# S5 scan in chunks: four units fed at once into eight banks, states read in pairs, and the gate in the same block

## The reference, cut to what matters

```python
bu_re = jnp.einsum('bsgh,gph->bsgp', uf, bb_re)
bu_im = jnp.einsum('bsgh,gph->bsgp', uf, bb_im)
_, _, xr, xi = lax.associative_scan(combine, (a_re_t, a_im_t, bu_re, bu_im), axis=1)
y = (jnp.einsum('bsgp,ghp->bsgh', xr, c_re)
     - jnp.einsum('bsgp,ghp->bsgh', xi, c_im))
y = y.reshape(bsz, seq, S5_WIDTH) + d_skip * uf.reshape(bsz, seq, S5_WIDTH)
y = jax.nn.gelu(y, approximate=False)
y = y * jax.nn.sigmoid(y @ w_glu + b_glu)
```

## Time and profile before

| | us |
|---|---|
| median of 3 timed runs | 2995.52 |
| lowest, highest | 2992.05, 3009.61 |
| profiled execution | 2989.28 |
| its span | 2987.5 |
| mean granted clock of TensorE in it | 0.955 |

### The profile page before, as it was taken

The page is one execution under the profiler, slowest core; times in us unless marked ns, Lnnn a source line. Parts: engine busy times, 40 slices in busy tenths (PEclk is TensorE's granted clock), DMA queues, the critical chain, the costliest instruction groups (busy, mean ns, idle before and its releaser), DMA issues. The chain is left out here.

```text
span 2987.5 us, 38641 instructions
## 1 busy us (share of the span) xinstructions
PE 2740.0 (92%) x14085; PEld 2295.0 (77%) x14085; DVE 1947.1 (65%) x3130; ACT 1037.2 (35%) x1635; POOL 1283.5 (43%) x607
## 2 busy tenths in 40 slices
PE   7998999778989998979988999998999969999996
PEld 5887877336778887758876789998999958888785
DVE  5444232683454444366555267778999969999998
ACT  4232321453233223222022233334655524444342
POOL 3443442002434443423042356773222247777773
PEclk9999999699999999989798999999999989999998
DMA  5443341002234443322002245557999999999993
GB/s 177 136 152 116 106 151 50 1 1 64 91 99 141 150 131 113 99 84 78 15 1 64 83 133 158 165 171 282 344 341 353 343 306 373 376 370 376 377 374 137
DMA packets 186680, 528.83 MB, mean 177 GB/s; under 512 B 14032, under 2 KB 96336, under 8 KB 166480
## 3 DMA queue, kind: packets, MB, share of 16 engines
q1 hardware_dynamic: 80208, 292.66, 30.4%
q0 software_dynamic: 18432, 134.23, 11.5%
q10 hardware_dynamic: 87936, 100.68, 9.8%
HBM read 475.08 MB, written 52.43 MB: 177 GB/s over the span
## 5 line engine op out<-in xcount | busy, mean ns | idle before, releaser
L344 POOL TENSOR_TENSOR ring_low<-ring,ring_high 128x1024 fp32r<-128x1024 f32 x323 | 795.0, 2464 | 1164.4 <-ACT ring_high L311 1164.4
L395 PE MATMUL ps<-u_high,ring_high 128*128 128x512 f32 (+1 forms) x1824 | 695.9, 382 | 44.5 <-DVE u_low L618 17.4
L396 PE MATMUL ps<-u_low,ring_high 128*128 128x512 f32 (+1 forms) x1824 | 686.9, 377 | 0.0
L397 PE MATMUL ps<-u_high,ring_low 128*128 128x512 f32 (+1 forms) x1824 | 686.3, 376 | 0.0
L311 ACT ACTIVATE ring_high<-ring 128x1024 fp32r<-128x1024 f32 x355 | 374.5, 1055 | 618.4 <-PE ps L397 549.4
L395 PEld LDWEIGHTS ps<-u_high,ring_high 128*128 128x128 f32 x1824 | 345.6, 189 | 111.3 <-issue 40.9
L396 PEld LDWEIGHTS ps<-u_low,ring_high 128*128 128x128 f32 x1824 | 346.1, 190 | 52.5 <-issue 2.0
L397 PEld LDWEIGHTS ps<-u_high,ring_low 128*128 128x128 f32 x1824 | 345.7, 190 | 52.6
L2346 POOL DMA_INDIRECT fetched_rows<-in_peer_uv,fetch_index x128 | 165.1, 1290 | 339.7 <-DVE ps L2366 302.4
L344 POOL TENSOR_TENSOR ring_low_more<-ring,ring_high_more 128x1024 fp32r<-128x1024 f32 x96 | 243.2, 2546 | 32.3 <-ACT ring_high_more L311 31.7
L2901 DVE TENSOR_TENSOR expert_coef_low<-expert_product,expert_coef_high 128x384 fp32r<-128x384 f32 x128 | 214.7, 1677 | 0.1
(11 more groups left out here) (427 smaller groups left out, 4863.4 us busy)
## 6 DMA issues: line engine op xcount, KB each, us to landing
ring<-in_peer_u SPq DMA_DIRECT2D x128, 512.0 KB
ring<-in_peer_uv SPq DMA_DIRECT2D x128, 512.0 KB
ring<-in_ffn_gu SPq DMA_DIRECT2D x88, 512.0 KB
ada_weights<-in_ada_w SPq DMA_DIRECT2D x48, 512.0 KB, 3.8
ring<-in_ffn_down SPq DMA_DIRECT2D x48, 512.0 KB
expert_acts<-kept_acts ACTq DMA_DIRECT2D x128, 192.0 KB, 4.0
expert_weights<-weight_stage ACTq DMA_DIRECT2D x24, 1024.0 KB, 8.9
group_acts<-expert_acts ACTq DMA_DIRECT2D x16, 1536.0 KB
```

The lines of the kernel that those rows point to most:

```text
L344: pool.tensor_tensor(k.lows[p], k.ring[:, s], k.highs[p].bitcast(F32), ALU.subtract)\
L395: pe.matmul(out, k.highs[p][:, w], high, start=first, stop=False)
L396: pe.matmul(out, k.highs[p][:, w], low, start=False, stop=False)
L397: last = pe.matmul(out, k.lows[p][:, w], high, start=False, stop=final)
```

## The change

- All four units are fed in one alternation, unit `r` into banks 2r and 2r + 1: eight banks. `fed.sem` is raised once.
- Lags go to bank 0, and so wait for state 1. Within writes banks 0 to 3; its third tile waits for state 2.
- Reads run tile by tile in pairs of units: 0 and 1 alternate, then, after state 4, 2 and 3 alternate. The states still have two places, so VectorE waits before unit 2's write for the end of the first pair's reads (`read.sem`).
- `s5_glu` is gone as a block. Skip, Gelu and gate stand in `s5_chunks`, tile by tile: the second pair's reads raise `done.sem` for each tile, then skip, Gelu and the tile's share of the gate's products follow. The products run over input tiles outside and the four banks 4 to 7 inside.
- `gates` follows the last skip on VectorE; `mark` follows the last read on GpSimd. `s5_x` serves as output of the gate.

```diff
                 def feed(r, a, at, c):
-                    rows, b = slice(32 * r, 32 * (r + 1)), r % 2
-                    return pe.matmul(k.ps[:, 2 * b + c, a * SPANS:(a + 1) * SPANS], s.feed[rows, SPAN - 1 - at, c, a],
+                    rows = slice(32 * r, 32 * (r + 1))
+                    return pe.matmul(k.ps[:, 2 * r + c, a * SPANS:(a + 1) * SPANS], s.feed[rows, SPAN - 1 - at, c, a],
                                      chunks(u[rows, a])[:, :, at], start=at == 0, stop=at == SPAN - 1)
...
-                def read_unit(r):
-
-                    rows = slice(32 * r, 32 * (r + 1))
-                    pe.wait_ge(state.sem, r + 1)
-                    for a in range(4):
-                        for at in range(SPAN):
-                            out = chunks(k.ps[rows, 4 + a])[:, 1:, at]
-                            for c in range(2):
-                                mm = pe.matmul(out, s.read[:, at + 1, c, 4 * r + a],
+                def read_states(units, a):
+
+                    for at in range(SPAN):
+                        for c in range(2):
+                            for r in units:
+                                rows = slice(32 * r, 32 * (r + 1))
+                                mm = pe.matmul(chunks(k.ps[rows, a])[:, 1:, at], s.read[:, at + 1, c, 4 * r + a],
                                                x[:, r % 2, c, a * SPANS:(a + 1) * SPANS - 1],
                                                start=False, stop=at == SPAN - 1 and c == 1)
-                    mm.then_inc(done.sem, 1)
+                    return mm
 
                 for a in range(4):
                     for at in range(SPAN):
                         for c in range(2):
-                            feed(0, a, at, c)
-                            mm = feed(1, a, at, c)
-                mm.then_inc(fed.sem, 2)
+                            for r in range(UNITS):
+                                mm = feed(r, a, at, c)
+                mm.then_inc(fed.sem, 1)
+                pe.wait_ge(state.sem, 1)
                 lags()
-                within()
-                for r in range(2):
-                    pe.wait_ge(state.sem, r + 1)
-                    feed_unit(r + 2)
-                    read_unit(r)
-                read_unit(2)
-                read_unit(3)
+                pe.wait_ge(placed.sem, UNITS)
+                for a in range(4):
+                    if a == 2:
+                        pe.wait_ge(state.sem, 2)
+                    within(a)
+                for a in range(4):
+                    mm = read_states((0, 1), a)
+                mm.then_inc(read.sem, 1)
+                pe.wait_ge(state.sem, 4)
+                for a in range(4):
+                    read_states((2, 3), a).then_inc(done.sem, 1)
+                pe.wait_ge(s.glu_loaded.sem, 16)
+                for a in range(4):
+                    pe.wait_ge(acted.sem, a + 1)
+                    for m in range(4):
+                        mm = pe.matmul(k.ps[:, 4 + m], s.glu_w[:, a, m * P:(m + 1) * P], u[:, a], start=a == 0, stop=a == 3)
+                        if a == 3:
+                            mm.then_inc(product.sem, 1)
...
+                for a in range(4):
+                    act.wait_ge(skipped.sem, a + 1)
+                    act.activation(u[:, a], u[:, a], ACT.Gelu).then_inc(acted.sem, 1)
...
-                    if r >= 2:
-                        dve.wait_ge(done.sem, r - 1)
-                    dve.tensor_tensor(x[:, b, 0], part[:, 0], both[:, 1], ALU.subtract)
-                    ins = dve.tensor_tensor(x[:, b, 1], part[:, 1], both[:, 0], ALU.add)
+                    if r == 2:
+                        dve.wait_ge(read.sem, 1)
+                    dve.tensor_tensor(x[:, r % 2, 0], part[:, 0], both[:, 1], ALU.subtract)
+                    ins = dve.tensor_tensor(x[:, r % 2, 1], part[:, 1], both[:, 0], ALU.add)
                     ins.then_inc(state.sem, 1)
                     dve.wait_ge(state.sem, r + 1)
-                dve.wait_ge(done.sem, UNITS)
                 for a in range(4):
-                    dve.scalar_tensor_tensor(u[:, a], u[:, a], k.vec("d_skip")[:, a:a + 1], k.ps[:, 4 + a],
-                                             ALU.mult, ALU.add)
+                    dve.wait_ge(done.sem, a + 1)
+                    dve.scalar_tensor_tensor(u[:, a], u[:, a], k.vec("d_skip")[:, a:a + 1], k.ps[:, a], ALU.mult, ALU.add)\
+                       .then_inc(skipped.sem, 1)
+                recurrence.gates(dve)
```

More of the change, by code:

```diff
@@ L2074, in turns_of_chunks, with s5_chunks @@
                 twice()
-def s5_chunks(k, s, u):
+def s5_chunks(k, s, u, x, recurrence):
     nc = k.nc
+    rounded = k.tiles_rounded
+    part = k.after
+    w = (k.total, k.rs)
+    out = x[:].rearrange("p b c t -> p (b c) t")
     with ExitStack() as tmp:
[L2084 to L2094, removed]
+        sem = lambda name: Signal(tmp, nc, name)
+        fed, state = sem("s5_chunks_fed"), sem("s5_states_ready")
+        lagged, cleared, placed = sem("s5_lags_multiplied"), sem("s5_lags_cleared"), sem("s5_lags_placed")
+        read, done, skipped = sem("s5_states_read"), sem("s5_tiles_multiplied"), sem("s5_skip_added")
+        acted, gated, product, mixed = (sem("glu_" + n) for n in ("gelu_ready", "gate_ready", "product_ready", "mixed"))
         chunks = lambda ap: ap.rearrange("p (c s) -> p c s", s=SPAN)
@@ L2173, in _ @@
                     rows = slice(32 * r, 32 * (r + 1))
-                    act.activation(s.lag[rows, :, :, rows], k.ps[rows, 7].rearrange("p (a l h) -> p a l h", a=4, l=SPAN),
+                    act.activation(s.lag[rows, :, :, rows], k.ps[rows, 0].rearrange("p (a l h) -> p a l h", a=4, l=SPAN),
                                    ACT.Copy).then_inc(placed.sem, 1)
+                for a in range(4):
+                    act.wait_ge(skipped.sem, a + 1)
+                    act.activation(u[:, a], u[:, a], ACT.Gelu).then_inc(acted.sem, 1)
+                for m in range(4):
+                    act.wait_ge(product.sem, m + 1)
+                    act.activation(out[:, m], k.ps[:, 4 + m], ACT.Sigmoid, bias=k.vec("glu_b")[:, m:m + 1])\
+                       .then_inc(gated.sem, 1)
+                    act.wait_ge(mixed.sem, m + 1)
+                    act.activation(k.u.high[:, 4 + m], out[:, m], ACT.Copy).then_inc(rounded.sem, 1)
             @block.vector
@@ L2180, in _ @@
                 tt = lambda o, a, b, op: step(dve.tensor_tensor(o, a, b, op))
+                dve.wait_ge(fed.sem, 1)
                 for r in range(UNITS):
-                    b = r % 2
-                    both = k.ps[:, 2 * b:2 * b + 2]
+                    both = k.ps[:, 2 * r:2 * r + 2]
                     turn = lambda n: s.turn[:, n, 4 * r:4 * r + 4].rearrange("p a t -> p (a t)")\
                         .unsqueeze(1).to_broadcast((P, 2, T))
-                    dve.wait_ge(fed.sem, r + 1)
                     step(dve.tensor_tensor(part[:], both, turn(0), ALU.mult))
@@ L2266, in mixer2 @@
             copy_tiles(k, k.dram["w_in_2"], 16, proj, k.u, beside=chunked)
[L2267 to L2268 removed]
+            states = k.sbuf("s5_x", [P, 2, 2, T], ctx=inner)
             recurrence = Recurrence(k, inner, proj, chunked)
[L2270 removed]
+            s5_chunks(k, chunked, state_in, states, recurrence)
             hgrn(k, recurrence)
```

62 lines of the change are left out of this document (10 added, 52 removed).

## The result

The changed kernel takes 2965.86 us, the median of 4 timed runs (2961.12 to 2966.26), beside 2993.78 us of the kernel before (2990.82 to 3009.61, 4 runs). The ratio is 0.9898, with a 95% interval of 0.9864 to 0.9932. The forecast was 2969.5, its range 2961 to 2985.

The account below looks back on a forecast made before the run. The prediction took one stretch to be bound by its serial path, later VectorE's four units: 118.4 us less 26.4 leaves 92, with 0.4 lost to the clock, so 26 off the median 2995.5 gives 2969.5 us; range 2961 to 2985.

Parts of the forecast that it names:

- the stage: Stretch from the first feed product to the next stage's first product; some 118 us before, forecast 92.3.
- both new waits: TensorE idle 10.4 us before lags; VectorE waiting 5.4 us for the first reads before writing unit 2's state.
- within: TensorE's products between lags and first reads; the old trace's 11.35 us was kept.
- feed, 256 records: Feed of all four units in alternation on four row groups: 14.9 us, as two units took before.
- VectorE's wait before unit 2's write: VectorE must wait 5.4 us for the first reads, with unit 3's whole chain queued behind.
- second reads: Reads of units 2 and 3 after 12 us of idle TensorE: 9.2 us, 4 of them at clock 0.50.
- gate loop and last rest: Tail from the first sigmoid: four ScalarE loops of 2.15 us and a last rest of 0.7, together 9.3.
- next stage's row: First row after the stretch: longer TensorE idling means more time at clock 0.50, costing some 0.4 us.
- Rival 1: In the feed only two row groups overlap: feed 29.8 us, saving 11, time 2984; chance 0.09.
- lag row: Trace row of the lags: four column groups, 64 records in 3.4 us, taken as evidence for fourfold overlap.
- Rival 2: Four feed groups at a factor near three: feed 19.8 us, time 2974; chance 0.12.
- A beat of one row group: Reading of the lone feed's 232 ns a record as one row group's fixed rate, independent of the clock.

Follow-up runs that it names:

- e1: Changed kernel with all four units still fed ahead of everything, but unit by unit instead of in alternation: 3008.53 us, one run.
- e2: Changed kernel with units 0 and 1 fed in alternation, then units 2 and 3, all ahead of VectorE's first turn: 2980.92 us, one run.
- e9: Changed kernel with feed products taking 128 neighbouring columns instead of every fourth, leaving out the order of time: 2957.2 us, one run.
- e4: Changed kernel with each feed product cut into two of 64 columns, twice the weight loads: 2970.49 us, one run.
- e6: Changed kernel with units 2 and 3's states in places of their own, so VectorE doesn't wait: 2957.90 us, median of 4.
- e5: Changed kernel with reads going unit by unit instead of in alternating pairs: 2975.86 us, one run.
- e8: Changed kernel with Gelu, gate, `gates` and `mark` back in a block of their own behind a barrier: 2973.39 us, one run.
- e3: As e2, but each pair signals for itself, so VectorE starts after the first pair: 2971.34 us, one run.
- e10: As e6 with four state places, but units 0 to 2 read in one alternation, then unit 3: 2961.03 us, one run.
- e11: As e10, with S5's input ordered by place in chunk; input copy, last rounding and rest turn the order: 2952.68 us, median of 4.
- e7: Changed kernel with unit 2 read alone as soon as its state is there, then unit 3: 2966.89 us, one run.
- e12: As e11, but the order is turned back once, in the skip: 2950.43 us, median of 6, ratio 0.9819.

## Why the prediction was right

The forecast was 26.4 us off the stage (118.7 to 92.3) and 0.4 lost in the next stage's first row, 26.0 together. Measured are 25.4 and 1.4, 24.0 together. The path and both new waits came as forecast; what was short is the clock, in three terms. Step by step, in us (VectorE's wait lies beside within and the first reads and isn't added):

| step | forecast | measured |
|---|---|---|
| feed, 256 records | 14.9 | 14.77 |
| unit 0 on VectorE, TensorE idle | 10.4 | 10.4 |
| lags to within | 6.3 | 6.30 |
| within | 11.35 | 12.72 |
| first reads | 7.1 | 7.13 |
| VectorE's wait before unit 2's write | 5.4 | 6.8 |
| writes and unit 3 | 11.8 | 11.8 |
| second reads | 9.2 | 9.70 |
| first gate product to the first sigmoid | 11.4 | 11.5 |
| gate loop and last rest | 9.3 | 8.8 |
| next stage's row, before 5.14 | 5.54 | 6.57 |

- **Feed.** Right in size; e1 and e2 measured what the rivals would have cost. Rival 1's 107.2 us (92.3 + 14.9) is e2's 107.1. The lag row was the right evidence for four groups, and the pair's factor of two held on. Rival 2 is refuted: 14.77 us where a beat a third longer gives 19.8. The estimate of 19.3 from the Trainium skill's factor of 3.07 ("TensorE: Matmul & The Clock Gate", section on measured speedup against the span model, for 512 columns) isn't borne out by these 128-column products, which take 14.77.
- **What lay behind the 232 ns** was read wrongly. "A beat of one row group" that doesn't hang on the clock was true as a number. Its cause is the 16-byte step (e9), and e4 refutes the weight loads. This hid the largest gain left, 7.2 us of the feed. That the step halves the rate at either clock, as I put it for e9, isn't shown: no run feeds neighbouring columns at 0.50, and the 212 ns of a column group of the lags at 0.50, without a step, speak against it.
- **Within and second reads** were mis-sized by 1.4 and 0.5 us, the clock alone: I had kept within's 11.35 us from the earlier trace rows, and now half of it runs at 0.50. The 10.4 us of idle time ahead of the lags are only part of the cause: e9 has them too, and its within takes 11.59. For the second reads I took 4 us at 0.50, and 5.3 came:

```profile
1474.20:1479.40 5.20, 5.20 (x50) 4.51 (x52) 0.50 0.01 3
1479.60:1483.60 4.00, 4.00 (x78) 4.00 (x75) 1.00 0.00 0
```

- **The wait of VectorE** was named, with its place. It is longer by what within is longer. e6 confirms that all of it is on the path.
- **The gate.** The loop's 2.15 us from the earlier trace rows is 1.99 to 2.05 now. From a sigmoid's start to its copy's end are 2.15 us still (1495.27 to 1497.42), but the next sigmoid starts 0.1 us ahead of the copy's recorded end, at 1497.32: records of one engine overlap, and the step has to be read from start to start. `gates`, masks and the table load are hidden, as forecast.
- **The next stage** lost 1.4 us to the clock (6.57 against 5.14), inside the bounds of 0 and 2, above the 0.4 taken.
- **From the stage to the time.** I added 6.2 us, the distance of the profiled execution before from its median. After, the distance is 0.05 us. The median came out 3.6 us below the forecast although the saving was 2.0 us short of it: the 6.2 us went away, the code ahead of the stage took 3.7 more and the code behind the next stage's first row 3.1 less. That the median came so near is in part luck; the stage is where the forecast was tested.

Where the 25.4 us come from can be put together from the runs. The pairs of reads are 13.2 (e5) and the gate in the same block 6.0 (e8), each taken away alone. Four instead of two units in alternation add 0.8 (e3). The rest, some 5.4 us (4.5 if the alternation is worth 1.7), would be for the feeds moved from between the reads to the front; it is a difference of the others, and no run has it alone. The 29.6 us of lone feeds bought so little because VectorE's four units, 10.4 us each, were under them, and are the path now.

Not tried: to let VectorE start on unit 0 while other units still feed, tile by tile; it would read banks that TensorE is writing.

## What to carry to other kernels

When work is packed together on one engine, look for what it had been hiding: here VectorE's scans came into the open, and two units early were nearly as good as four. Read a matmul's rate with its operand's step in mind: here a rate that didn't change with the clock had its limit at the operand, and one copy that reads with the step, made where its engine waits anyway, took the step out of the feed and of within. A gap's price is its length and what the clock loses behind it; it can pay to fill it with work that was never late.

## What the runs showed of the hardware that I hadn't expected

- **A 16-byte step in TensorE's moving fp32 operand** costs a factor of two at clock 1.00: 14.77 against 7.53 us for 256 records of 128 columns (e9). At 0.50 no cost can be seen, though only tiles of another shape can be compared: 216 ns a record with the step in e1, and 53 x 4 = 212 without it for a group of the lags. The same step in the PSUM output costs nothing at 1.00: 7.12 us for 64 records with it (e10) and without it (e11).
- **Four row groups** run side by side with hardly a loss, 57.7 ns a record; three column groups cost no more than two (e10).
- **The clock** stays at 1.00 through the fourfold feed; a lone feed (e1) had fallen to 0.50 by 1416.0, 4.9 us after its start, although TensorE has no idle time there, and in pairs (e3) it runs at 0.50 from 1417 to 1440. Idle gaps of 3.2 us left it at 1.00 (e7, e10); behind gaps of 4.23 (e11) and 5.05 us (e6) it was 0.50. Equal gaps don't give equal losses: behind 11.8 us the second reads take 8.87 (e3), 8.98 (e9) or 9.70 us (base).
- **A step on the elementwise engines** cost 0.35 to 0.45 us for 128x512 fp32 elements: ScalarE's copy 0.63 to 1.08 and VectorE's `tensor_tensor` 0.69 to 1.04, both with an SBUF input at a step of 512 bytes (e11), and VectorE's skip 0.75 to 1.14, with a PSUM input and an SBUF output at a step of 16 bytes (e12). VectorE's copy that only reads PSUM at a step of 16 bytes took its usual 0.69.
